# W_out's attention part in four pieces of 512 columns, with additions and first FFN products reordered around the last piece

## What is computed

```python
mixed = jnp.concatenate([rms_norm(y_lru, lru_out_g), rms_norm(y_attn, attn_out_g)], axis=-1)   # 512 + 512
x = x + mixed @ w_out                                   # 1024 x 1024
hf = rms_norm(x, ffn_norm_g)
up = causal_depthwise_conv(hf @ w_up, ffn_conv_w, ffn_conv_b)   # 1024 x 5632
gate, val = jnp.split(up, 2, axis=-1)
x = x + (jax.nn.gelu(gate) * val) @ w_down              # 2816 x 1024
```

## Time and profile before

| | |
|---|---|
| median of three runs | 289.66 us (289.46 to 289.79) |
| the profiled execution | 289.71 us, span 288.0 us |
| busy: PE / PEld / DVE / ACT / POOL | 283.4 / 246.3 / 242.7 / 201.0 / 11.4 us |
| granted clock of TensorE, mean | 1.00 |
| HBM read / written | 50.98 / 1.05 MB |

### The profile page before, as it was taken

The page is one execution under the profiler, slowest core; times in us unless marked ns, Lnnn a source line. Parts: engine busy times, 40 slices in busy tenths (PEclk is TensorE's granted clock), DMA queues, the critical chain, the costliest instruction groups (busy, mean ns, idle before and its releaser), DMA issues.

```text
span 288.0 us, 4994 instructions
## 1 busy us (share of the span) xinstructions
PE 283.4 (98%) x1642; PEld 246.3 (86%) x1642; DVE 242.7 (84%) x448; ACT 201.0 (70%) x389; POOL 11.4 (4%) x26
## 2 busy tenths in 40 slices
PE   7999999999999999999999999999999999999996
PEld 7688999898788999888888888888888888888885
DVE  2998898889999888999887788888888888887775
ACT  4893599999897687777567656655775566567640
POOL 3000004600000000000000000000000000000000
PEclk9999999999999999999999999999999999999999
DMA  7999950330365715374748445463746644200004
GB/s 282 423 421 420 394 196 1 148 145 14 135 228 211 250 44 167 126 291 162 278 147 277 164 164 220 167 193 137 287 146 200 237 146 166 125 0 2 0 0 146
DMA packets 8112, 52.25 MB, mean 181 GB/s; under 512 B 928, under 2 KB 1312, under 8 KB 2080
## 3 DMA queue, kind: packets, MB, share of 16 engines
q1 hardware_dynamic: 7920, 51.50, 48.0%
q0 software_dynamic: 176, 0.53, 0.5%
HBM read 50.98 MB, written 1.05 MB: 181 GB/s over the span
## 4 chain that ended last, share of the span: by engine, by line
PE 95%; DMA 2%; DVE 1%; ACT 1%; SPq 0%; issue 0%
PE bank L1420 25%; PE bank L1062 15%; PE bank L1063 14%; PE bank L1066 14%; PE bank L1429 13%; PE bank L1118 3%; PE bank L1372 3%; DMA x_tok<-in_x_dram 2%; PE bank L1383 1%; PE bank L1182 1%; PE bank L1306 1%; PE bank L1213 1%; PE bank L1222 1%; PE bank L1176 1%; PE bank L1339 1%; DVE w_hi L691 0%
## 5 line engine op out<-in xcount | busy, mean ns | idle before, releaser
L703 DVE TENSOR_TENSOR w_lo<-raw,w_hi 128x1024 fp32r<-128x1024 f32 x93 | 110.9, 1220 | 10.1 <-ACT w_hi L381 9.6
L381 ACT ACTIVATE w_hi<-raw 128x1024 fp32r<-128x1024 f32 x83 | 84.0, 1055 | 0.3
L1420 PE MATMUL bank<-h_both,w_hi 128*128 128x512 f32 x320 | 76.0, 389 | 0.0
L1420 PEld LDWEIGHTS bank<-h_both,w_hi 128*128 128x128 f32 x320 | 59.9, 188 | 12.4
L1429 PEld LDWEIGHTS bank<-h_both,w_lo 128*128 128x128 f32 x320 | 41.2, 191 | 1.6
L1429 PE MATMUL bank<-h_both,w_lo 128*128 128x256 f32 x320 | 41.7, 283 | 0.0
L614 ACT ACTIVATE tanh_a<-bank 128x256 f32<-128x256 f32 x44 | 16.5, 376 | 34.6 <-PE bank L1429 34.6
L622 ACT ACTIVATE xc<-ygate,par 128x256 f32<-128x256 f32 x44 | 26.5, 601 | 15.5 <-DVE ygate L985 15.5
L1062 PE MATMUL bank<-w_hi,act_hi 128*128 128x512 f32 (+1 forms) x90 | 34.8, 387 | 0.0
L1063 PE MATMUL bank<-w_lo,act_hi 128*128 128x512 f32 (+1 forms) x90 | 34.8, 387 | 0.0
L1066 PE MATMUL bank<-w_hi,act_lo 128*128 128x512 f32 (+1 forms) x90 | 34.6, 384 | 0.0
(11 more groups left out here) (193 smaller groups left out, 410.9 us busy)
## 6 DMA issues: line engine op xcount, KB each, us to landing
raw<-in_stream_dram SPq DMA_DIRECT2D x47, 1024.0 KB, 4.8
x_tok<-in_x_dram SPq DMA_DIRECT2D x2, 512.0 KB, 5.0
out_dram<-x_tok SPq DMA_DIRECT2D x3, 256.0 KB, 2.1
p_T<-in_gates_dram POOLq DMA_DIRECT2D x1, 512.0 KB, 9.4
out_dram<-x_tok SPq DMA_DIRECT2D x2, 128.0 KB, 2.1
par<-in_params_dram SPq DMA_DIRECT2D x1, 117.0 KB, 6.5
mix_g<-in_params_dram POOLq DMA_DIRECT2D x1, 4.0 KB, 5.6
```

Source lines behind the costliest of these rows:

```text
L381: act.activation(hi_tile(u)[:, :], raw_unit(u), ACT.Copy).then_inc(hi_done, 1)
L703: dve.tensor_tensor(w_lo[u % RING][:, :], raw_unit(u), hi_tile(u)[:, :].bitcast(F32), ALU.subtract).then_inc(lo_done, 1)
L1420: pe.matmul(acc[:, :], whi[:, kc, :], h_both[:, kc, :, :].rearrange("p b t -> p (b t)"), start=kc == 0, stop=False)
```

## The change

A_PIECES has four entries in place of five: the last two, of 256 columns in banks 5 and 7, become one of 512 in bank 5. With it go one ScalarE square, and VectorE's second mean; for each half of the tokens the mean now takes the first piece's sum, and the Sqrt's own operand the second's. VectorE adds the last piece behind five instead of six f_parts, and the mean of piece 2 comes ahead of the f_parts. TensorE takes transpose_f(0) in after two of the last piece's four units instead of ahead of its own piece; gate0 and value0 run chunks 0 to 4 each, and 5 to 7 by turns; and the first two matmuls of value1, with the wait for unit 31's high part, stand ahead of transpose_f(1).

```diff
--- before.py
+++ after.py
@@ -177,7 +177,7 @@
         q_scale = small[:, 76:80]
         out_rms, out_rstd, out_ss = small[:, 80:84], small[:, 84:88], small[:, 88:92]
         y_rstd, a_rstd = out_rstd[:, 0:TT], out_rstd[:, TT:2 * TT]
-        f_ss, f_sum, f_rms, f_rstd = small[:, 200:205], small[:, 94:96], small[:, 96:98], small[:, 98:100]
+        f_ss, f_sum, f_rms, f_rstd = small[:, 200:204], small[:, 94:96], small[:, 96:98], small[:, 98:100]
         lam_p = small[:, 100:104]
         x_part, x_mean = small[:, 206:207], small[:, 207:208]
         warm_out = small[:, 1:2]
@@ -258,8 +258,7 @@
         Y_PIECES = ((0, slice(0, 512), bank[0][:, 0:512]), (0, slice(512, 1024), bank[1][:, 0:512]),
                     (1, slice(0, 512), bank[6][:, 0:512]), (1, slice(512, 1024), bank[7][:, 0:512]))
         A_PIECES = ((0, slice(0, 512), bank[2][:, 0:512]), (0, slice(512, 1024), bank[3][:, 0:512]),
-                    (1, slice(0, 512), bank[4][:, 0:512]), (1, slice(512, 768), bank[5][:, 0:256]),
-                    (1, slice(768, 1024), bank[7][:, 0:256]))
+                    (1, slice(0, 512), bank[4][:, 0:512]), (1, slice(512, 1024), bank[5][:, 0:512]))
         DOWN = (bank[4], bank[5], bank[2], bank[3])
 
 
@@ -577,8 +576,8 @@
                                accum_out=f_ss[:, i:i + 1]).then_inc(f_sq, 1)
 
             def f_norm(m):
-                last = (1, len(A_PIECES) - 1)[m]
-                act.wait_ge(f_added, (1, 3)[m])
+                last = 2 * m + 1
+                act.wait_ge(f_added, m + 1)
                 act.wait_ge(f_sq, last + 1)
                 act.activation(f_rms[:, m:m + 1], f_ss[:, last:last + 1], ACT.Sqrt, bias=f_sum[:, m:m + 1],
                                scale=1.0 / D_MODEL).then_inc(f_rms_done, 1)
@@ -602,7 +601,6 @@
             for kc in range(KC):
                 f_part(0, kc)
             f_square(3)
-            f_square(4)
             f_norm(1)
             for kc in range(KC):
                 f_part(1, kc)
@@ -937,13 +935,8 @@
 
                 m = A_PIECES[i][0]
                 dve.wait_ge(f_sq, i + 1)
-                if i in (0, 2):
-                    dve.tensor_scalar(f_sum[:, m:m + 1], f_ss[:, i:i + 1], 1.0 / D_MODEL, EPS, ALU.mult,
-                                      ALU.add).then_inc(f_added, 1)
-                else:
-                    dve.wait_ge(f_added, 2)
-                    dve.scalar_tensor_tensor(f_sum[:, m:m + 1], f_ss[:, i:i + 1], 1.0 / D_MODEL, f_sum[:, m:m + 1],
-                                             ALU.mult, ALU.add).then_inc(f_added, 1)
+                dve.tensor_scalar(f_sum[:, m:m + 1], f_ss[:, i:i + 1], 1.0 / D_MODEL, EPS, ALU.mult,
+                                  ALU.add).then_inc(f_added, 1)
 
             def f_norm(m):
                 dve.wait_ge(f_rms_done, m + 1)
@@ -965,14 +958,12 @@
             los(U_FFN + 1)
             f_norm(0)
             f_add(2)
+            f_mean(2)
+            for kc in range(5):
+                f_part(0, kc)
             f_add(3)
-            for kc in range(6):
+            for kc in range(5, KC):
                 f_part(0, kc)
-            f_add(4)
-            f_part(0, 6)
-            f_part(0, 7)
-            f_mean(2)
-            f_mean(3)
             f_norm(1)
             hi(U_SPARE + 1)
             for kc in range(KC):
@@ -1349,7 +1340,7 @@
                 if i == 3:
                     pe.wait_ge(out_summed, 2 * TT)
                 for j in range(LC, KC):
-                    if i == 4 and j == LC:
+                    if i == 3 and j == LC + 2:
                         transpose_f(0)
                     ins = a_piece(U_O + j, i)
                     if i == len(A_PIECES) - 1:
@@ -1385,17 +1376,21 @@
                 ins.then_inc(unit_used, 1)
 
             gate0, value0 = early_high(0, 0, 0), early_high(0, 1, 0)
-            for chunks in (range(6), (6, 7)):
+            for high in (gate0, value0):
+                for kc in range(5):
+                    high(kc)
+            for kc in range(5, KC):
                 for high in (gate0, value0):
-                    for kc in chunks:
-                        high(kc)
+                    high(kc)
             pe.wait_ge(x2_done, len(A_PIECES))
             gate1 = early_high(1, 0, 0)
             for kc in range(KC):
                 gate1(kc)
+            value1 = early_high(1, 1, 0)
+            value1(0)
+            value1(1)
             transpose_f(1)
-            value1 = early_high(1, 1, 0)
-            for kc in range(KC):
+            for kc in range(2, KC):
                 value1(kc)
             gate0, value0 = early_high(0, 0, 1), early_high(0, 1, 1)
             for kc in range(KC):
```

## The result

The changed kernel takes **290.34 us**, median of 14 runs (290.14 to 290.49), against 289.72 us (289.46 to 289.84) for the kernel before: ratio 1.0022, 95% interval 1.0016 to 1.0029. The forecast was 290.35 us in a range of 289.75 to 290.85, slower with a chance of 0.65. The interval lies wholly above 1, so the changed kernel is slower. The difference of 0.62 us (0.46 to 0.84 by the interval) is just over the 0.58 us, 0.2%, that the prediction took as the least it calls slower, and the interval holds that line.

What follows compares the result with a forecast made beforehand. The prediction took TensorE, busy 98% of the span, to bound the kernel. A shift of +0.66 us at value1, with the pieces' 0.13 already inside, plus 0.02 behind it gave +0.68 and 290.35 us, range 289.75 to 290.85.

Steps and rivals of the forecast that it cites:

- The pieces give 0.13 us: On TensorE, 24 matmuls of 256 columns (2.86 us) become 12 of 512 (2.73 us): 0.13 us gained, all on the path.
- No wait for transpose_f(0), f_mean(2) costs nothing: TensorE's first transposes at 98.98 find inputs and bank ready; VectorE's f_mean(2) ends by 99.6, before f_part starts at 99.87.
- The bank that the prediction has all eight transposes wait for: For transpose_f(0) on TensorE, the bank is free at 98.65, when VectorE's L933 ends, before the transposes at 98.98.
- f_add(3) from 101.43, h_lo up to 0.2 us late: VectorE's last addition runs 101.43 to 102.18; h_lo for chunk 5 follows at 102.43, so TensorE waits about 0.2 us.
- the same data was wanted 0.4 us later: At gate0 and value0, the kernel before wanted h_lo of chunks 5 to 7 0.4 us later than the changed one.
- The cast ends at 104.71: VectorE's cast of unit 31's high part, behind f_norm(1), runs from 104.02 to 104.71; TensorE wants it at 103.99 or 104.2.
- value1(0) counts from 104.9, shift 0.66: TensorE stands until the cast ends, resuming at 104.90 against 104.24 before: +0.66 us, bounds 0.5 and 0.85.
- Behind it 0.02 us: At down(0), the act_lo chain shifted by 0.90 meets TensorE shifted by 0.66, 119.81 against 119.86: 0.02 us taken.
- h_lo at 108: Second half's last h_lo comes at 108.12, TensorE's load at 108.30: fits by 0.18. Rival that such margins fail: chance 0.13.
- Sum +0.68: Whole kernel: +0.66 us at value1 and +0.02 us behind it, +0.68 us in all.
- the near end of its own case: Own case runs from 290.15 to 290.6 us, chance 0.70; a quarter of it lies within 0.58 us, counted as no difference.
- The rival in which the cast is no obstacle: Unit 31's cast is through by about 104.15 us, so value1 doesn't wait: 289.5 to 289.8 us, not slower, chance 0.14.

Runs made afterwards that it cites:

- experiment 5: Changed kernel with VectorE's cast of unit 31 ahead of f_mean(2), and value1(0), value1(1) ahead of chunks 5 to 7 of gate0 and value0: 289.63 us, ratio 0.9998.
- experiment 8: The kernel of experiment 5, plus ScalarE's copy ffn_cross(0, 1) put ahead of the high part of a later unit: 289.57 us, ratio 0.9995.
- experiment 7: The kernel of experiment 1, with transpose_f(0) ahead of the last piece in place of in its middle: 290.36 us, ratio 1.0023.
- experiment 2: Kernel before, with only value1(0) and value1(1) moved ahead of transpose_f(1): 290.21 us, ratio 1.0019.
- experiment 3: Changed kernel with VectorE's cast of unit 31 moved ahead of f_mean(2), the reader staying ahead of transpose_f(1): 289.85 us, ratio 1.0005.
- experiment 6: Changed kernel with four value1 matmuls ahead of transpose_f(1) in place of two: 290.66 us, ratio 1.0034.
- experiment 1: Changed kernel with all eight value1 matmuls back behind transpose_f(1): 289.71 us, ratio 1.0002.

## Why the prediction was right

Point by point, by its own steps:

- *The pieces give 0.13 us.* 0.12 to 0.14, seen in experiments 5 and 8, where nothing covers it: from the last piece to the first product 3.62 us (97.81 to 101.43) where before has 3.74 (97.78 to 101.52), and 0.14 over the whole stretch. No run has the wider pieces alone in the kernel before. The formula of the Trainium skill ("TensorE: Matmul & The Clock Gate", section "Back-to-back issue gap") would have had 0.03. The Trainium skill gives it there for an isolated matmul, which the prediction leaves out, and about 131 ns at 512 columns for a stream of loads and matmuls. The trace agrees with neither: 227 ns at 512 columns and 119 to 120 at 256, which is 12 to 14 ns over N/2.4. The measurement decides.
- *No wait for transpose_f(0), f_mean(2) costs nothing.* Both so. f_mean(2) is in the idle time ahead of the f_parts. The bank that the prediction has all eight transposes wait for is wanted by the last two alone: in experiment 7 they start at 98.21, while the addition that reads it runs until 98.67. That changes nothing in its sum.
- *f_add(3) from 101.43, h_lo up to 0.2 us late.* From 101.38, on a trace that runs 0.05 ahead, and 0.21. That "the same data was wanted 0.4 us later" before is misread: chunk 5 was wanted at 101.84 then and was ready by 101.51; what was wanted later was chunk 6, the first behind an addition there (load at 102.68 against 102.31). The sum doesn't use it.
- *The cast ends at 104.71.* 103.98 + 0.69 = 104.67, with the same 0.05.
- *value1(0) counts from 104.9, shift 0.66.* From 104.83, and 0.64 in the chain. Of the release I took the upper part; it was 0.05 to the load and 0.11 from load to matmul, the two values of the earlier trace rows, in each run that waits for the cast (0.04 to 0.05 for the first).
- *Behind it 0.02 us.* 0.06: the term was named with its margin of 0.05 and sized too small. The hand-over to TensorE, which the margin had to hold too, took the rest: from the end of act_lo to the load it is 0.11 us here (119.75 to 119.86) and 0.11 to 0.12 in experiments 2, 3, 5 and 6, not the 0.05 behind the cast. h_lo at 108 had its slack, and lost it in experiment 6, as its margin says.
- *Sum +0.68.* The trace has +0.70, the medians +0.62.

The mechanism is shown; the closeness of the numbers is in part luck. The forecast was a shift of 0.69 us from a median of 289.66, the measured shift is 0.62 from 289.72, and the two misses cancel to 0.01 in 290.34 against 290.35. By the prediction's own line of 0.58 us the result is slower by 0.04 only, and the near end of its own case would have been no difference. It put that line at a cast 0.08 us earlier than reckoned; by its whole sum, with the 0.02 behind it, it is 0.10 to 0.11. The rival in which the cast is no obstacle is what experiments 1 and 3 build: 289.71 and 289.85 us, inside or just beyond the 289.5 to 289.8 it was given.

## What to carry to other kernels

When a product is moved ahead as a filler, list every operand it waits for and look where each is made: h_lo of the two chunks was there by 100.4 us, four microseconds before (VectorE's five from 99.75, 0.26 apart), but the weight's high part stood in another engine's queue behind the very chain that the filler was to bridge. There was no wait to fill at that place (experiment 1), and the filler made one of half a microsecond; moving one line in VectorE's queue took it away. A larger piece saved a little of TensorE's time, but what is behind it becomes ready later and all at once; here 0.13 us of gain met 0.20 us of waiting until other work was put between.

## What I had not expected

- How additive it is: eight edits around a queue that is 98% busy came out within about 0.1 us of sums made from single rows, and the distance in the chain told differences of 0.06 us that the times (intervals of about 0.25 us to each side for most runs) can't.
- act_lo at 119 us hangs on the transposes at 105 with no slack between. From the last piece's first matmul to the transposes the changed kernel takes 7.50 us (97.73 to 105.23 in the chain) and the one before 6.62 (to 101.52 + 2.88), +0.88; from that same matmul to the start of act_lo 21.60 (to 119.33) and 20.71 (to 118.49), +0.89. VectorE and ScalarE carry the delay over 14 us undiminished, and one copy put ahead on ScalarE frees it: in experiment 8 act_lo ends 0.58 us ahead of TensorE's load.
